# From the fifth dilated head on: the embedding's projection ahead of the feed-forward, two gate tiles out of their loop, down slabs in pairs, the last slab in parts

## The reference

```python
u = rmsnorm(x, g_mix) @ w_in             # conv branch (3 x 512 columns), q, k, v of 8 heads of 64
c = gated causal conv of width 3         # 512 channels
o = dilated attention(q, k, v)           # three dilations, one softmax over all of them
x = x + concat(rmsnorm(c), rmsnorm(o)) @ w_out
h = rmsnorm(x, g_ffn)
gate, up = h @ w_gate, h @ w_up          # 2816 = 22 tiles of 128
x = x + (silu(causal_conv3(gate)) * up) @ w_down
e = p @ w_ple_proj                       # p: an embedding of 256 columns per token, an input
x = x + sigmoid(rmsnorm(x, g_ple) @ w_ple_gate) * e
```

## Time and profile before

| | |
|---|---|
| median of 3 runs | 1813.9 us (1813.67 to 1814.55) |
| the profiled execution | 1814.2 us |
| its span, first to last instruction | 1812.4 us |
| PE busy | 1773.6 us, 98% |
| DVE, ACT busy | 983.6 us (54%), 668.3 us (37%) |
| chain that ended last | PE 89%, DVE 5%, ACT 4%, issue 1%, DMA 1% |

### The profile page before, as it was taken

One profiled execution on the slowest core, in us unless ns is written; L12 is line 12 of the kernel. 1 busy time (PEld: TensorE's weight loads), 2 busy tenths in 40 slices (PEclk: granted clock), 3 DMA queues, 4 the chain that ended last, 5 costly groups with the idle time before them and its releaser, 6 DMA issues.

```text
span 1812.4 us, 23486 instructions
## 1 busy us (share of the span) xinstructions
PE 1773.6 (98%) x9636; PEld 1510.2 (83%) x9636; DVE 983.6 (54%) x1433; ACT 668.3 (37%) x938; POOL 1.9 (0%) x11
## 2 busy tenths in 40 slices
PE   9999999999999999999999999999998999999998
PEld 7777998888889988998888889888787788888886
DVE  3666663334347666753434347657566665356554
ACT  3445442313134576441313233434354232222332
POOL 0000000000000000000000000000000000000000
PEclk9899999999999999999999999999999999999999
DMA  8211232222322221223222223112111223322341
GB/s 283 93 52 42 94 117 93 93 96 90 116 85 101 72 71 66 76 81 105 93 93 94 91 97 113 55 62 93 47 71 58 94 103 122 122 93 93 116 151 59
DMA packets 28597, 169.74 MB, mean 94 GB/s; under 512 B 2848, under 2 KB 7392, under 8 KB 9440
## 3 DMA queue, kind: packets, MB, share of 16 engines
q1 hardware_dynamic: 22592, 156.44, 24.2%
q10 hardware_dynamic: 5920, 12.08, 2.0%
HBM read 166.39 MB, written 5.27 MB: 95 GB/s over the span
## 4 chain that ended last, share of the span: by engine, by line
PE 89%; DVE 5%; ACT 4%; issue 1%; DMA 1%; DVEq 0%; SPq 0%; ACTq 0%
PE ps L1664 29%; PE ps L1666 27%; PE ps L1665 27%; DVE w_lo L888 2%; PE ps L1797 2%; ACT w_hi L419 1%; DMA stage<-slabs 1%; PE ps L1776 1%; PE ps L2010 0%; ACT y L576 0%; PE ps L2142 0%; PE ps L1737 0%; ACT act_hi L581 0%; PE ps L1917 0%; PE ps L1728 0%
## 5 line engine op out<-in xcount | busy, mean ns | idle before, releaser
L1664 PE MATMUL ps<-act_hi,w_lo 128*128 128x512 f32 (+1 forms) x1504 | 545.9, 363 | 14.6 <-issue 4.4
L1666 PE MATMUL ps<-act_lo,w_hi 128*128 128x512 f32 (+1 forms) x1504 | 538.7, 358 | 0.0
L1665 PE MATMUL ps<-act_hi,w_hi 128*128 128x512 f32 (+1 forms) x1504 | 538.7, 358 | 0.0
L419 ACT ACTIVATE w_hi<-stage 128x2048 fp32r<-128x2048 f32 (+4 forms) x147 | 267.5, 1820 | 378.4 <-PE ps L1666 377.2
L888 DVE TENSOR_TENSOR w_lo<-stage,w_hi 128x2048 fp32r<-128x2048 f32 (+6 forms) x152 | 322.5, 2123 | 85.8 <-ACT w_hi L419 78.9
L1664 PEld LDWEIGHTS ps<-act_hi,w_lo 128*128 128x128 f32 x1504 | 284.4, 189 | 62.5 <-issue 13.8
L1666 PEld LDWEIGHTS ps<-act_lo,w_hi 128*128 128x128 f32 x1504 | 284.3, 189 | 42.3
L1665 PEld LDWEIGHTS ps<-act_hi,w_hi 128*128 128x128 f32 x1504 | 284.4, 189 | 40.1
L1664 PE MATMUL ps<-hid_hi,w_lo 128*128 128x512 f32 (+1 forms) x608 | 218.4, 359 | 2.1 <-DVE w_lo L888 2.1
L1666 PE MATMUL ps<-hid_lo,w_hi 128*128 128x512 f32 (+1 forms) x608 | 216.9, 357 | 0.0
L1665 PE MATMUL ps<-hid_hi,w_hi 128*128 128x512 f32 (+1 forms) x608 | 215.3, 354 | 0.0
(11 more groups left out here) (293 smaller groups left out, 2172.2 us busy)
## 6 DMA issues: line engine op xcount, KB each, us to landing
stage<-slabs SPq DMA_DIRECT2D x147, 1024.0 KB, 4.8
bias_rows<-bias_line ACTq DMA_DIRECT2D x1, 3072.0 KB, 15.2
strips<-dilated ACTq DMA_DIRECT2D x2, 1024.0 KB, 4.8
out<-y ACTq DMA_DIRECT2D x4, 512.0 KB, 2.6
y<-x_t ACTq DMA_DIRECT2D x3, 512.0 KB, 8.8
strips<-bias_rows ACTq DMA_DIRECT2D x1, 1024.0 KB, 5.6
strips<-bias_rows ACTq DMA_DIRECT2D x2, 512.0 KB, 4.2
stage<-slabs SPq DMA_DIRECT2D x3, 256.0 KB, 8.6
```

What stands on the lines that cost most here:

```text
L419: nc.scalar.activation(w_hi[p][:, 0:w], stage[s][:, 0:w], ACT.Copy).then_inc(cast_hi, 1)
L1664: mm(out, l_lo, r_hi, start=start, stop=False, skip_group_check=shared)
L1665: mm(out, l_hi, r_hi, start=False, stop=False, skip_group_check=shared)
L1666: return mm(out, l_hi, r_lo, start=False, stop=stop, skip_group_check=shared)
```

## The change

The arithmetic stays the same. Instructions move, and some tiles are cut otherwise:

1. Dilated stretch. ACT and DVE cast slab MIX_OUT after the root and the inversion for `k1` and not before. PE does `mix_tile(0)` ahead of the scores of head 4, and DVE adds it to `y` ahead of head 4's bias. Slab MIX_OUT + 1 is cast before the loop over heads 4 to 7, by DVE thus ahead of the bias of head 5.
2. The projection is slab 105 now, ahead of the feed-forward, in five parts (tiles 0-1, 2, 3, 4-5, 6-7), each as soon as DVE has read those banks. ACT takes all of it out of PSUM (`proj_part`). The embedding's low part is made by POOL and not by DVE. The casts of the first gate slabs FFN_A, FFN_A + 1 and FFN_A + 2 stand in other places on both engines. Round B has no projection any more.
3. The first two gate tiles of round A stand ahead of the loop, on ACT and DVE.
4. Down slabs 0 and 1 of each round are one piece of work on PE: all but the last two k-steps of slab 0, the same of slab 1, then the last two of slab 0, and of slab 1.
5. The first PLE_GATE slab no longer waits for the last down tile's read. The last one is done in three parts, a tile of 512 tokens and two halves of a tile, each with its own scaling, sigmoid, sum and store.

```diff
-FFN_A, FFN_A_DOWN = 105, 117
-FFN_B, FFN_B_DOWN = 125, 136
-PLE_PROJ = 135
+PLE_PROJ = 105
+FFN_A, FFN_A_DOWN = 106, 118
+FFN_B, FFN_B_DOWN = 126, 136
...
...
+            pool.wait_ge(p_split, 1)
+            nc.gpsimd.tensor_tensor(p_lo[:, :, :], p_raw[:, :, :], p_hi[:, :, :].bitcast(F32), ALU.subtract)\
+                .then_inc(p_split, 1)
...
-                cast(g + p + 2)
-                root("qk"[p] + str(half), 16)
+                if half and p:
+                    root("k1", 16)
+                    cast(g + p + 2)
+                else:
+                    cast(g + p + 2)
+                    root("qk"[p] + str(half), 16)
...
             exps(dil, d_prob, 4)
+            cast(MIX_OUT + 1)
             for u in range(4, 8):
                 dil_head(u)
-                if u == 4:
-                    cast(MIX_OUT + 1)
...
+            act.wait_ge(dil.biased, 4 * 8)
+            act.dma_start(p_raw[:, :, :], ple_t).then_inc(p_landed, 16)
...
-            for j in range(4):
-                g = MIX_ATT + j // 2
-                rms_out(*((slab_read, g + 1) if j % 2 else (part_read, 10 + j // 2)), [2 * j, 2 * j + 1], j, "g_ffn")
-                if j % 2:
-                    cast(g + 2)
...
+            def proj_part(n):
+                t, m = PROJ_PARTS[n]
+                b = att_bank(t)
+                if n < 4:
+                    act.wait_ge(proj_done, n + 1)
+                else:
+                    act.wait_ge(slab_done, PLE_PROJ + 1)
+                nc.scalar.activation(proj[:, t:t + m, :], ps[:, b:b + m, :], ACT.Copy)\
+                    .then_inc(proj_read if n < 4 else slab_read, 1)
+            cast(PLE_PROJ)
+            rms_out(part_read, 10, [0, 1], 0, "g_ffn")
+            act.wait_ge(p_landed, 16)
+            nc.scalar.activation(p_hi[:, :, :], p_raw[:, :, :], ACT.Copy).then_inc(p_split, 1)
+            rms_out(slab_read, MIX_ATT + 1, [2, 3], 1, "g_ffn")
+            rms_out(part_read, 11, [4, 5], 2, "g_ffn")
+            cast(FFN_A)
+            for n in range(3):
+                proj_part(n)
+            rms_out(slab_read, MIX_ATT + 2, [6, 7], 3, "g_ffn")
+            for n in range(3, 5):
+                proj_part(n)
+            cast(FFN_A + 1)
+            cast(FFN_A + 2)
             root("ffn")
...
-            act.wait_ge(proj_half, 1)
-            for q in range(2):
-                last = nc.scalar.activation(proj_a[:, 2 * q:2 * q + 2, :], ps[:, 2 * q:2 * q + 2, :], ACT.Copy)
-            last.then_inc(proj_act, 1)
-            cast(PLE_PROJ + 2)
...
-            for j in range(4):
...
+            for n, (m, c) in enumerate(LAST_PARTS):
+                act.wait_ge(last_read, n + 1)
+                nc.scalar.activation(gate_in[:, 1, m, c], gate_in[:, 1, m, c], ACT.Sigmoid).then_inc(sig_done, 1)
+                if n:
+                    m, c = LAST_PARTS[n - 1]
+                    act.wait_ge(out_ready, 3 + n)
+                    act.dma_start(out[:, 6 + m, c], y[:, 6 + m, c]).then_inc(stored, 16)
+            m, c = LAST_PARTS[2]
+            act.wait_ge(out_ready, 6)
+            act.dma_start(out[:, 6 + m, c], y[:, 6 + m, c]).then_inc(stored, 16)
```

DVE's own changes, PE's and the order of the slabs:

```diff
-            cast(MIX_OUT)
             mean_squares("k1", 6, 1.0, 16)
             invert_root("k1", 16)
+            cast(MIX_OUT)
             qk_full_out(1, 1)
             qk_lo(1, 1)
             conv_out(3)
             dve.wait_ge(dil_ready, 3 + 1)
             v_out(1)
             dve.wait_ge(strips_landed, 16 * 4)
+            mix_tile(0)
             dil_bias(4)
-            mix_tile(0)
             divide(dil, d_prob, 4)
             mix_tile(1)
+            cast(MIX_OUT + 1)
...
+                if j == 0:
+                    cast(PLE_PROJ)
+                elif j == 3:
+                    cast(FFN_A)
                 rms_out([2 * j, 2 * j + 1], j, "g_ffn", SQUARED["ffn"])
-                if j % 2:
-                    cast(g + 2)
+            cast(FFN_A + 1)
             mean_squares("ffn", 7, 1.0)
             invert_root("ffn")
+            cast(FFN_A + 2)
             dve.wait_ge(rstd_ready, RSTD["ffn"])
```

```diff
+            for n, (m, c) in enumerate(LAST_PARTS):
+                part = gate_in[:, 1, m, c]
+                dve.wait_ge(last_done, n + 1)
+                nc.vector.tensor_tensor(part, ps[:, last_bank(n), 0:c.stop - c.start], rstd[:, c], ALU.mult)\
+                    .then_inc(last_read, 1)
+                dve.wait_ge(sig_done, 3 + n + 1)
+                link(nc.vector.tensor_tensor(part, part, proj[:, 6 + m, c], ALU.mult))
+                nc.vector.tensor_tensor(y[:, 6 + m, c], y[:, 6 + m, c], part, ALU.add).then_inc(out_ready, 1)
...
+            mix_tile(0)
             pe.wait_ge(slab_read, g + 3)
             pe.wait_ge(dil_ready, 3 + 2)
             score(dil, 4, dil_operands, 4)
-            mix_tile(0)
...
+            s = place(PLE_PROJ)
+            pe.wait_ge(cast_lo, PLE_PROJ + 1)
+            pe.wait_ge(p_split, 2)
+            for n, (t, m) in enumerate(PROJ_PARTS):
+                if t in (0, 4):
+                    pe.wait_ge(part_read, 10 + t // 4)
+                else:
+                    pe.wait_ge(slab_read, MIX_ATT + 1 + t // 4)
+                for x in range(t, t + m):
                     for k in range(2):
-                        c = (k * KT + m) * P
-                        last = product(ps[:, m, :], w_hi[s][:, c:c + P], w_lo[s][:, c:c + P], p_hi[:, k, :],
-                                       p_lo[:, k, :], k == 0, k == 1)
-                    if m == 3:
-                        last.then_inc(proj_half, 1)
-                last.then_inc(slab_done, 1)
+                        c = (k * KT + x) * P
+                        last = product(ps[:, att_bank(x), :], w_hi[s][:, c:c + P], w_lo[s][:, c:c + P],
+                                       p_hi[:, k, :], p_lo[:, k, :], k == 0, k == 1)
+                last.then_inc(proj_done if n < 4 else slab_done, 1)
...
+                    pe.wait_ge(proj_read, 4)
                     plain(first, ready=act_tiles(FFN_X))
...
-                if rnd:
-                    ple_projection()
-                for j in range(8):
-                    def hidden(k):
-                        pe.wait_ge(h_ready, before + k + 1)
-                    if rnd and j == 0:
-                        pe.wait_ge(proj_act, 1)
-                    plain(down + j, kt=count, hi=h_hi, lo=h_lo, ready=hidden if j == 0 else None, n=1)
+                for k0, k1 in ((0, count - 2), (count - 2, count)):
+                    for g in (down, down + 1):
+                        if k0 == 0:
+                            pe.wait_ge(slab_read, g - 1)
+                            pe.wait_ge(cast_lo, g + 1)
+                        for k in range(k0, k1):
+                            pe.wait_ge(h_ready, before + k + 1)
+                            last = product(ps[:, banks(g), :], w_hi[place(g)][:, k * P:(k + 1) * P],
+                                           w_lo[place(g)][:, k * P:(k + 1) * P], h_hi[:, k, :], h_lo[:, k, :],
+                                           k == 0, k == count - 1)
+                        if k0:
+                            last.then_inc(slab_done, 1)
+                for j in range(2, 8):
+                    plain(down + j, kt=count, hi=h_hi, lo=h_lo, n=1)
...
-                plain(PLE_GATE + j, ready=act_tiles(PLE_X) if j == 0 else steps, free=PLE_GATE if j < 2 else None)
+                plain(PLE_GATE + j, ready=act_tiles(PLE_X) if j == 0 else steps)
...
+            s, g = place(PLE_GATE + 3), PLE_GATE + 3
+            pe.wait_ge(slab_read, g - 1)
+            pe.wait_ge(cast_lo, g + 1)
+            for n, (m, c) in enumerate(LAST_PARTS):
+                for k in range(KT):
+                    w = (k * 2 + m) * P
+                    last = product(ps[:, last_bank(n), 0:c.stop - c.start], w_hi[s][:, w:w + P], w_lo[s][:, w:w + P],
+                                   act_hi[:, k, c], act_lo[:, k, c], k == 0, k == KT - 1)
+                last.then_inc(last_done, 1)
```

135 lines of the change are left out of this document (65 added, 70 removed).

## The result

The changed kernel takes 1816.0 us (median of 20 runs, 1812.1 to 1819.2), the kernel before 1813.2 (20 runs, 1810.3 to 1814.8). The ratio is 1.0015, with a 95% interval of 1.0009 to 1.0022: a little slower, where the forecast had a little faster.

The account below looks back on a forecast made before the run. PE, busy for 98% of the 1812.4 us span, was taken to bound the kernel. Gains of 16.5 us against losses of 15.4 summed to -1.1, giving 1812.8 us as the median, range 1807 to 1818.

Parts of the forecast that it names:

- dilated stretch: PE between 1286 and 1324 us: the new order removes idle time and two clock falls, 7.2 us gained.
- transition: Attention half to third gate slab: the projection fills PE's waits and POOL's subtraction stays hidden, 4.7 us gained.
- gate tiles out of the loop: Round A's first two gate tiles ahead of the loop: no cost, as PE has 2 us of slack per tile.
- first PLE_GATE slab: Start of the embedding's gate slabs: the wait of 0.78 us goes, 0.9 us gained.
- down slabs in pairs, waits: Down slabs of both rounds: late casts make PE idle, 3.8 us lost in A and 7.4 in B, together 11.2.
- clock after them: Behind the paired down slabs' new waits: clock falls at 1.4 us each, 4.2 us lost.
- last slab in parts: Kernel's end: shorter steps and a smaller store after the last matmul, 3.7 us gained.
- The rival with POOL and DVE in each other's way: Attention half to third gate slab: the engines hinder each other, gain there 2.5 us or less, time 1815; chance 0.07.
- The rival in which the dilated stretch gives nothing: Between 1286 and 1324 us: thin matmuls and DVE's lag lose the 7.2 us again, time 1820; chance 0.15.
- the held clock: Rival: PE's new idles cost no clock at all, time 1807.2 us; chance 0.3.
- the early cast of slab 1: Rival: down slab 1's cast comes before PE wants it, 5.1 us lost in place of 11.2, time 1804.6; chance 0.03.
- The rival's idea that thin matmuls bring the clock down: Scores' matmuls on 64 rows, not the waits, cause both clock falls between 1286 and 1324 us; within a rival of chance 0.15.

Follow-up runs that it names:

- that part alone: The kernel before with only the new order of the dilated part, all else as before: 1806.4 us, ratio to before 0.9948 to 0.9976.
- the early copy: The changed kernel with ACT copying the embedding's high part right after its load, so POOL's subtraction falls where DVE waits: 1813.5 us.
- waits filled: The changed kernel with useless matmuls (9, 9, 15 and 15) put into PE's four new waits in the down slabs: 1811.4 us.
- last slab whole: The changed kernel with unpaired down slabs, ACT copying the embedding's high part earlier, and the last PLE_GATE slab undivided: 1804.0 us, against 1799.4 in parts.

## Why the prediction was wrong

The sum was -1.1 us, and the two profiled executions are 3.7 apart: 4.8 too little. The medians went up by 2.8: 3.9 too little. By its own terms (traces, with the projection's 48 matmuls at the 11.22 us from 1691.59 to 1702.81):

| step | predicted | traced | shown by |
|---|---|---|---|
| dilated stretch | -7.2 | -7.3 | that part alone: -7.2 |
| transition | -4.7 | -3.0 | -5.0 with the early copy |
| gate tiles out of the loop | 0 | 0 | round A's gate slabs from the third on: 108.9 and 108.8 us |
| first PLE_GATE slab | -0.9 | -0.9 | the trace |
| down slabs in pairs, waits | +11.2 | +11.4 | waits filled; a trace without falls |
| clock after them | +4.2 | +7.2 | the same |
| last slab in parts | -3.7 | -3.8 | last slab whole: 3.7 |

The first row holds 0.3 us of chance: where the two programs are still the same, at the first of the 2-column matmuls, the changed kernel's trace is at 1286.12 and before's at 1285.81.

The dilated stretch: its result held, and mix tile 3 has no wait. Its working had one error: a fall at the earlier trace rows was priced at 1.4 us by counting all rows that touch the window. Steps at half clock are 0.43 us against 0.229, so 3.4 us lose 1.6:

```profile
1526.87 0.63 PE L1712 MATMUL ps<-h_hi,w_lo 128*128 128x512 f32 x1
1527.30 0.63 PE L1713 MATMUL ps<-h_hi,w_hi 128*128 128x512 f32 x1
1527.72 0.63 PE L1714 MATMUL ps<-h_lo,w_hi 128*128 128x512 f32 x1
```

**The clock term failed**, by 3.0 us in the profiled execution. It counted three falls of 1.4. That execution has four, three of 3.4 us and one of 5.5, together 15.7 us; by the steps they lose 7.3, by the phases 7.2. So both the number of falls and the price of one were too low. The number is luck in part: 8 of 12 short waits brought the clock down, which is too few cases to tell from the half that was assumed. Over all executions the term is less sure: filling the waits gave 4.6 by the medians and 5.3 by the ratios, with about 2 us either way, so how much of the medians' miss is the clock's stays open.

**The transition's term failed**, by 1.7 us. Its own list of steps is right, and with the subtraction elsewhere it gives 5.0. The failing sentence is that POOL's subtraction is hidden: the prediction looked at when PE wants `p_lo`, not at what runs beside it on DVE. The rival with POOL and DVE in each other's way, given 0.07, was this, with a price of 2.2 us against 1.9 measured. It came along with the forecast's case and did not replace it. How much it takes depends on who comes first: in the trace of the filled waits, where two of DVE's instructions did, the transition lost only 0.5.

The pairing, the largest and, with its clock, the only costly term, was right in its waits: 2.00 and 2.13 us against 2.2 and 2.4, 3.41 and 3.59 against 3.6 and 3.8. So it is shown where the gain of the other steps went: without pairing the changed kernel is 15.2 us faster. By the medians the two failed terms and the waits' 0.2 leave about 1 to 1.6 of the 3.9 us to no step; that lies within their intervals.

The rival in which the dilated stretch gives nothing is refuted, as are the held clock and the early cast of slab 1. Open is why the clock sometimes holds after a wait of 2.0 us: two executions of the same waits differ, and no run here was made to tell them apart. The rival's idea that thin matmuls bring the clock down was not tested by itself; two traces have a fall behind thin matmuls with no wait, and one has the scores' thin matmuls and their waits with no fall.

## What to carry to other kernels

Before you split accumulations so that two outputs share the wait for the last operand, look whether the engine that frees and refills the weights' places has slack: here it had none, and the split put the cast of the second slab and the release of the first on the path. Together with the projection's move that made 11 us of waits. Price a new wait of a busy TensorE as its length plus a little under half of the time at half clock that follows (here 1.6 us for 3.4). When work goes to an idle GpSimd, look at which two-operand instruction of VectorE runs beside it, and put it into VectorE's idle time.
